# Experts 2 and 3 get their slot lists on chip, and their gathers move in between the record scatters

## The reference

```python
g_w, g_idx = top_k(softmax(xt @ w_group + b_group), 1)          # 1 group of 4
e_w, e_idx = top_k(softmax(logits of that group's 4 experts), 2) # 2 experts of the group
for e in range(16):
    h = silu(xt @ w_gate[e]) * (xt @ w_up[e])                    # 1024 -> 512
    y = y + combine[:, e:e+1] * (h @ w_down[e])                  # 512 -> 1024
x = layer_norm(alpha * x + y)
```

## Time and profile before

| | us |
|---|---|
| median of 3 runs | 676.99 |
| the profiled execution, its own time | 675.32 |
| its span, first to last instruction | 673.5 |
| PE busy | 612.2 (91%) |
| DVE busy | 485.7 (72%) |
| ACT busy | 375.9 (56%) |
| POOL busy | 93.7 (14%) |
| an `elo` (128x2048 on DVE, line 1592), mean of 96 | 2.289 |
| an `ehi` (128x2048 on ACT, line 1227), mean of 96 | 1.917 |
| weight load of 1 MB, issue to landing, median | 7.0 to 7.6 |
| gather of 128 rows, issue to landing, median of 16 | 9.5 |

### The profile page before, as it was taken

The page is one execution under the profiler, slowest core; times in us unless marked ns, Lnnn a source line. Parts: engine busy times, 40 slices in busy tenths (PEclk is TensorE's granted clock), DMA queues, the critical chain, the costliest instruction groups (busy, mean ns, idle before and its releaser), DMA issues. The chain is left out here.

```text
span 673.5 us, 9730 instructions
## 1 busy us (share of the span) xinstructions
PE 612.2 (91%) x3731; PEld 495.3 (74%) x3731; DVE 485.7 (72%) x550; ACT 375.9 (56%) x393; POOL 93.7 (14%) x67
## 2 busy tenths in 40 slices
PE   9998999999999999999595999999999999999700
PEld 7787788887767888877474888888888888888500
DVE  3668698874448335446974889888898888888368
ACT  4567325522216666123374678777777887877411
POOL 0023033540000000000551011111111111100012
PEclk9999999999999999999797999999999999999955
DMA  9633111134005003935598799999999999973063
GB/s 334 234 127 124 59 69 63 63 114 86 1 13 177 1 1 131 415 133 184 180 424 360 252 367 405 392 391 394 387 396 383 404 395 399 398 299 115 27 256 123
DMA packets 42845, 152.83 MB, mean 227 GB/s; under 512 B 12995, under 2 KB 13203, under 8 KB 30524
## 3 DMA queue, kind: packets, MB, share of 16 engines
q1 hardware_dynamic: 37788, 139.70, 55.4%
q0 software_dynamic: 5024, 12.68, 4.8%
HBM read 143.87 MB, written 12.68 MB: 232 GB/s over the span
## 5 line engine op out<-in xcount | busy, mean ns | idle before, releaser
L1592 DVE TENSOR_TENSOR w_lo<-ring,w_hi 128x2048 fp32r<-128x2048 f32 x96 | 218.3, 2289 | 28.0 <-ACT w_hi L1227 27.8
L577 PE MATMUL psum<-w_hi,act_hi 128*128 128x512 f32 x544 | 221.0, 406 | 2.0 <-ACT ring L1139 1.9
L579 PE MATMUL psum<-w_hi,act_lo 128*128 128x512 f32 x544 | 213.1, 392 | 0.0
L578 PE MATMUL psum<-w_lo,act_hi 128*128 128x512 f32 x544 | 213.1, 392 | 0.0
L1227 ACT ACTIVATE w_hi<-ring 128x2048 fp32r<-128x2048 f32 x96 | 182.3, 1917 | 28.0 <-PE psum L579 28.0
L577 PEld LDWEIGHTS psum<-w_hi,act_hi 128*128 128x128 f32 x544 | 102.8, 189 | 28.0 <-issue 3.8
L579 PEld LDWEIGHTS psum<-w_hi,act_lo 128*128 128x128 f32 x544 | 102.5, 188 | 22.3
L578 PEld LDWEIGHTS psum<-w_lo,act_hi 128*128 128x128 f32 x544 | 102.8, 189 | 18.8
L1354 DVE TENSOR_TENSOR w_lo<-ring,w_hi 128x2048 fp32r<-128x2048 f32 x17 | 41.8, 2462 | 33.7 <-ACT w_hi L1076 33.6
L1076 ACT ACTIVATE w_hi<-ring 128x2048 fp32r<-128x2048 f32 x17 | 32.5, 1914 | 42.8 <-PE psum L579 41.0
L577 PE MATMUL psum<-act_hi,w_hi 128*128 128x512 f32 x128 | 51.6, 403 | 0.4 <-DVE w_lo L1372 0.4
(11 more groups left out here) (218 smaller groups left out, 678.1 us busy)
## 6 DMA issues: line engine op xcount, KB each, us to landing
ring<-in_w_gate SPq DMA_DIRECT2D x32, 1024.0 KB, 7.5
ring<-in_w_up SPq DMA_DIRECT2D x32, 1024.0 KB, 7.6
ring<-in_w_down SPq DMA_DIRECT2D x32, 1024.0 KB, 7.0
ring<-in_w_in SPq DMA_DIRECT2D x13, 1024.0 KB, 5.3
ring<-in_w_o SPq DMA_DIRECT2D x4, 1024.0 KB, 5.0
ring<-pair_dram SPq DMA_DIRECT2D x8, 512.0 KB, 7.5
ring<-in_x SPq DMA_DIRECT2D x2, 1024.0 KB, 6.3
ring<-strip_dram SPq DMA_DIRECT2D x8, 256.0 KB, 4.5
```

The source lines that it names most:

```text
L577: pe.matmul(dst, lh, rh, start=first, stop=False, skip_group_check=True)
L578: pe.matmul(dst, lh, rl, start=False, stop=False, skip_group_check=True)
L579: return pe.matmul(dst, ll, rh, start=False, stop=last, skip_group_check=True)
L1592: dve.tensor_tensor(w_lo[:, v0 % WBUF, :], ring[:, slot, :], w_hi[:, v0 % WBUF, :].bitcast(F32), ALU.subtract).then_inc(s_lo, 1)
```

## The change

Experts 2 and 3 (a new constant `EARLY = 4` is the first expert without) get their lists on chip as well. Their one-hot matrices and records use tiles that lie free then; PE's eight small matmuls for them stand between unit 2 and unit 3 and write to bank 6. On POOL, `gather(2)` stands behind five of the eight record scatters, with a wait for the new lists, and `gather(3)` behind seven. The read back from DRAM leaves out experts 2 and 3, and the loop over experts no longer gathers them. On PE `keep_warm(10, 4)` is gone. On DVE `elo(1)` moves behind the two halves of the lo part of expert 0's rows; `place(2)` and `place(3)` come between `elo(2)` and `elo(3)`, and `slots_of(2, 4)` behind `elo(3)`, ahead of `token_weights` and `elo(4)`. PE's first down unit waits for the new lists to have been read (`s_slots` 3), since it writes bank 6.

```diff
+EARLY = 4
-        one_hot = [act_hi[:, 5, :], act_hi[:, 6, :]]
+        one_hot = [act_hi[:, 5, :], act_hi[:, 6, :], act_hi[:, 7, :], act_lo[:, 5, :]]
 # POOL
+            def scatter_record(n):
+                i, k = n // 2, n % 2
+                pool.indirect_dma_start(out=slot_dram, ... addr_i[:, i, k:k + 1] ..., in_=rec_i[:, i, k, :], in_offset=None).then_inc(s_slotw, 16)
-            for i in range(T):
-                for k in range(2):
-                    pool.indirect_dma_start(out=slot_dram, ...).then_inc(s_slotw, 16)
+            for n in range(2 * T):
+                if n == 5:
+                    pool.wait_ge(s_slots, 3)
+                    gather(2)
+                if n == 7:
+                    gather(3)
+                scatter_record(n)
             pool.wait_ge(s_slotw, 16 * 2 * T)
-            pool.dma_start(slots[:, 2:NE, :], ...[:, 2:NE, :]).then_inc(s_slotd, 16)
+            pool.dma_start(slots[:, EARLY:NE, :], ...[:, EARLY:NE, :]).then_inc(s_slotd, 16)
             pool.wait_ge(s_slotd, 16)
             for e in range(NE):
-                if e + 2 < NE:
+                if EARLY <= e + 2 < NE:
                     gather(e + 2)
 # PE
-                    last = pe.matmul(psum[:, (5, 3)[e], 2 * e:2 * e + 2], ...)
+                    last = pe.matmul(psum[:, (5, 3, 6, 6)[e], 2 * e:2 * e + 2], ...)
                 if s0 > 1:
                     pe.wait_ge(s_y, s - 1)
                 else:
-                    pe.wait_ge(s_slots, 1)
+                    pe.wait_ge(s_slots, 3)
-            keep_warm(10, 4)
             pe.wait_ge(s_xtlofirst, 1)
             in_unit(2, 0, 0, 0, 0)
 ...
             in_unit(3, 0, 0, 2, 0)
+            for e in range(2, EARLY):
+                placed(e)
             in_unit(3, 0, 1, 3, 0)
 # DVE
             elo(0, 0)
-            elo(1, 0)
 ...
             dve.tensor_tensor(e_lo[:, 0, 512:1024], ...).then_inc(s_etlo, 1)
+            elo(1, 0)
             elo(2, 0)
+            place(2)
+            place(3)
             elo(3, 0)
+            slots_of(2, EARLY, 6)
             token_weights()
             elo(4, 0)
             xt_lo(1, 1)
```

More of the change, by code:

```diff
@@ L523, in gather @@
                                         in_offset=bass.IndirectOffsetOnAxis(ap=slots[:, e, 0:1].bitcast(U32), axis=0)).then_inc(s_xg[e % 2], 16)
+            def scatter_record(n):
+                i, k = n // 2, n % 2
+                pool.indirect_dma_start(out=slot_dram, out_offset=bass.IndirectOffsetOnAxis(ap=addr_i[:, i, k:k + 1].bitcast(U32), axis=0),
+                                        in_=rec_i[:, i, k, :], in_offset=None).then_inc(s_slotw, 16)
             pool.wait_ge(s_slots, 1)
@@ L532, in _ @@
             pool.wait_ge(s_addr, 1)
-            for i in range(T):
-                for k in range(2):
-                    pool.indirect_dma_start(out=slot_dram, out_offset=bass.IndirectOffsetOnAxis(ap=addr_i[:, i, k:k + 1].bitcast(U32), axis=0),
-                                            in_=rec_i[:, i, k, :], in_offset=None).then_inc(s_slotw, 16)
+            for n in range(2 * T):
[5 more added lines that the diff above has]
+                scatter_record(n)
             pool.wait_ge(s_slotw, 16 * 2 * T)
-            pool.dma_start(slots[:, 2:NE, :], slot_dram[0:P * NE, :].rearrange("(p e) r -> p e r", e=NE)[:, 2:NE, :]).then_inc(s_slotd, 16)
+            pool.dma_start(slots[:, EARLY:NE, :], slot_dram[0:P * NE, :].rearrange("(p e) r -> p e r", e=NE)[:, EARLY:NE, :]).then_inc(s_slotd, 16)
             pool.wait_ge(s_slotd, 16)
             for e in range(NE):
-                if e + 2 < NE:
+                if EARLY <= e + 2 < NE:
                     gather(e + 2)
@@ L944, in placed @@
                 for i in range(T):
-                    last = pe.matmul(psum[:, (5, 3)[e], 2 * e:2 * e + 2], one_hot[e][:, i * P:(i + 1) * P], record[:, i, e, :],
+                    last = pe.matmul(psum[:, (5, 3, 6, 6)[e], 2 * e:2 * e + 2], one_hot[e][:, i * P:(i + 1) * P], record[:, i, e, :],
                                      start=(i == 0), stop=(i == T - 1), skip_group_check=True)
```

## The result

The changed kernel takes 669.73 us (median of 4 runs, 667.83 to 670.03) against 677.44 for the kernel before (median of 4 runs; the 676.99 that the forecast starts from is of the first three): 7.7 us less, ratio 0.9879, 95% interval 0.9857 to 0.9901. Forecast were 668.5, that is 8.5 us less, range 665.5 to 673.5. The profiled execution took 670.03 us, with a span of 668.2.

What follows compares the result with a forecast made beforehand. PE, busy nearly throughout, was taken as the bound, with time to gain only where it idles or runs at half clock. Expert 2 starting 6.0 us earlier plus 2.5 us of half clock gave 676.99 - 8.5 = 668.5 us, range 665.5 to 673.5.

Steps and rivals of the forecast that it cites:

- The gather's wait and the half clock behind it: PE's 7.6 us wait for expert 2's gather and 2.5 us of half clock: 10.1 us at most to gain.
- The half clock behind the wait: Expert 2's first transposes and matmuls after PE's idle time run at clock 0.50, costing 2.5 us.
- The clock rises as before: At PE's start, the clock goes from 0.50 to 1.00 near 333.5 us even without the warm-up matmuls.
- the rival that I gave 0.22: Without warm-up matmuls PE's clock rises later at the start: 7.1 us saved, 669.9 us; chance 0.22.
- DVE's new wait, 2.2 us, and PE's, 1.9: After elo(3), DVE waits about 2 us for the small matmuls; PE then waits 1.9 us for xt_lo(1) before step 1.
- The gather lands with 3 to 12 us to spare: Expert 2's rows arrive between 347.7 and 356.6 us, before PE asks at 359.75.
- POOL's rest and the weights cost nothing: Later scatters, the read back near 363 us and shifted weight loads make nobody wait: no cost.
- The sum: Expert 2's transposes start 6.0 us earlier and 2.5 us of half clock go: 8.5 us saved, 668.5 us.
- the ten matmuls: PE's warm-up at the start, 2.23 us, was hidden in the wait before unit 0; removing it gives nothing.

Runs made afterwards that it cites:

- e2: The changed kernel with the ten warm-up matmuls back and elo(1) again ahead of the two halves of expert 0's lo part: 669.9 us, ratio 0.9884.
- e1: The changed kernel, unaltered, measured again: 669.52 us, ratio 0.9879 to the kernel before.
- e9: The kernel before with the warm-up matmuls gone and elo(1) behind the two halves, nothing early; second measurement of e3: 676.2 us, ratio 0.9981.
- e3: The kernel before with the warm-up matmuls gone and elo(1) behind the two halves, nothing early: 675.38 us, ratio 0.9968.
- e12: The kernel before, unaltered, measured and profiled again: 677.14 us, ratio 0.9993.
- e10: The kernel before with only elo(1) moved behind the two halves, warm-up matmuls kept: 677.44 us, ratio 0.9990.
- e5: The changed kernel with the eight small matmuls before unit 2, plus three of the ten warm-up matmuls: 664.52 us, ratio 0.9827 to the kernel before.
- e6: The changed kernel with the eight small matmuls before unit 2, second measurement of e4: 666.11 us, ratio 0.9841 to the kernel before.
- e8: The changed kernel with slots_of(2, 4) on DVE behind xt_lo(1) instead of ahead of token_weights: 665.86 us, ratio 0.9851 to the kernel before.
- e11: The kernel before with only the ten warm-up matmuls taken out: 675.79 us, ratio 0.9980.
- e7: The changed kernel with both early gathers behind all eight record scatters: 668.25 us, ratio 0.9876 to the kernel before.
- e4: The changed kernel with PE's eight small matmuls ahead of unit 2 instead of behind it: 665.98 us, ratio 0.9831 to the kernel before.

## Why the prediction was right

- *The gather's wait and the half clock behind it are nearly all of the gain*: right. The early lists alone, with the old start, give 7.9 us by medians (e2); the whole change gives 8.3 beside them (e1). The new start without early lists gave 1.3 and 2.2 by the ratios (e9, e3), where I had no term for it; on top of the early lists it adds nothing measurable. The half clock behind the wait was put at 2.5 us (5.47 less 2.9 is 2.6). From x2 to the span's end the kernel before takes 307.7 us and the changed one 305.4: it was 2.3.
- *The clock rises as before*: this step of the sum failed, and the rival that I gave 0.22 took its place. Forecast was a rise at t0 + 3.8, measured 7.1, 6.1 and 5.8. The half clock is worth 0.45 us per us here, so the 3.3 us of delay in the profile of the changed kernel cost 1.5; I had priced it at 1.4. The rival's time was 669.9, measured are 669.73 and 669.52. The 3.8 came from a single execution: the kernel before, profiled again, rose at 5.9.
- *DVE's new wait, 2.2 us, and PE's, 1.9*: measured 2.85 and 1.72. The order of events was as laid out; the small matmuls took 0.94 us in all.
- *The gather lands with 3 to 12 us to spare*: 7.3. It was issued at t0 + 15.3; I had 13.8.
- *POOL's rest and the weights cost nothing*: right. The read back moved from t0 + 21.8 to t0 + 34.4 and nobody waited for it, and from 362.7 on PE has no idle time.
- *The sum*: laid out for a rise at t0 + 3.8, x2 was to be 30.0. Carrying 0.45 us per us back from the measured 31.01 gives 29.5. So the rest of the chain was right to 0.5 us, and by luck in the direction that hid a part of the late rise. In the profiles the gain is 7.3 us where 8.5 were forecast, with 1.0 of the difference in x2 and 0.2 in the second half clock; by the medians it is 7.7.

What the warm-up matmuls have to do with the rise, the falls in the table tell. In the kernel before the clock fell at 326.7, between two of its stretches; in e12 it was 0.50 until 336.0 with PE busy throughout. Columns as in the earlier trace rows; two lines of the kernel before, then two of e12:

```profile
325.60:326.60 1.00, 0.00 (x0) 0.00 (x0) 0.90 (x5) 0.00 (x0) 0.90 (x1) 1.00 0.00 0
326.70:329.70 3.00, 0.00 (x0) 0.00 (x0) 2.73 (x12) 0.22 (x1) 1.99 (x2) 0.50 0.68 242
```

```profile
330.20:336.00 5.80, 5.80 (x23) 4.68 (x24) 5.80 (x5) 1.20 (x2) 5.19 (x3) 0.50 0.61 119
336.10:340.00 3.90, 3.90 (x18) 3.21 (x18) 0.61 (x1) 1.92 (x1) 3.29 (x3) 1.00 0.99 414
```

Where the fall came 3.1 to 3.8 us ahead of t0, the rise came at 3.1 to 3.8 with matmuls between the transposes and unit 0 (before, e10, e5), at 6.5 to 7.1 with the hole of 0.56 us (after, e6, e8), and at 10.0 with a hole of 2.14 us (e11). Where the fall came 4.1 to 4.7 us ahead, the rise came at 5.5 and 5.9 with the matmuls (e2, e12) and at 5.8 to 6.1 with the hole (e1, e3, e7, e9): hardly a difference. In e4 (fall at 5.0, with the hole) it came at 8.6. So the ten matmuls, which I had called worth nothing because unit 0 waited for DVE all the same, had a second use, but only in some executions; the rest of the delay is when the clock fell, ahead of all that the change touches. That the hole is the cause in the first group rests on seven profiles; of the times, those of e5 and e6 alone bear on it.

## What to carry to other kernels

Before an on-chip way replaces a way through DRAM, look at what stands behind the new wait in an in-order queue: here one instruction of 0.16 us cost 2 us of the gain, and moving it behind the two operations that PE was waiting for, or its producer ahead of a 2.8 us unit, gave them back. Matmuls that only keep PE busy need not be worthless because PE waits there anyway, and need not be worth their place either: three that fill the hole and are no longer than it brought x2 forward by 1.65 us (e5, by medians 1.6 us, by ratio not clear), while the kernel before became some 1 us faster without its ten (e11). And do not take the time of one clock rise from one profile: two of the same kernel had it 2.1 us apart. Count a gain from a point that the change does not touch, since the clock's stretches elsewhere move single profiles by 2 us.

## What the runs showed that I had not expected

An indirect DMA that POOL starts to issue while DVE is in an `elo` (a `tensor_tensor` on two SBUF operands) ends its issue 0.85 us after that operation, whenever it began: in the changed kernel the scatter of 348.29 ends at 350.81 and the `elo` of 347.67 at 349.96, the scatter of 351.12 ends at 354.13 and the `elo` before it (351.01 + 2.28) at 353.29. With DVE idle it takes 0.97. In the 14 profiles, between 318 and 375 us, 93 indirect DMAs begin beside an `elo`, and 92 of them end 0.83 to 0.90 us after it (the other began 0.01 us after the `elo` itself and took 1.01). A direct DMA of POOL is not held up: the read back of the lists took 0.59 us in all 14, and in 8 of them it began beside an `elo`, as in e7 above (349.24, the `elo` runs from 348.67 to 350.95). The Trainium skill (SBUF — State Buffer, "A bandwidth-pool intuition that's wrong") has a DMA issued by GpSimd blocked until about 0.1 us past the end of a `tensor_copy` of DVE. For the indirect DMAs here the direction agrees, the 0.85 us is what these rows show; for the direct one beside a `tensor_tensor` they show no wait. Through the indirect ones, what PE does at the start reaches POOL's chain: PE late, `elo` late, scatters quick. A gather issued earlier need not land earlier either: issued at t0 + 26.0 beside an `elo` (e11) it took 10.2 us, at t0 + 27.7 with DVE idle (before) 8.3.
